# Two transformer blocks on one core: index scores in split precision, a re-dealt recurrence, shared PSUM banks and a reordered merge

## What is computed

```python
# the choice of keys in layer 0: 16 index heads of width 64
rel = jax.nn.relu(jnp.einsum('bqhd,bsd->bqhs', qii, k_idx) * (IDX_DIM ** -0.5))
score = jnp.einsum('bqhs,bqh->bqs', rel, wi)
_, sel = lax.top_k(score, n_keep)            # n_keep = 128
# the recurrence of the second block, per head and direction (a = running sum of log forget gates)
decay = jnp.exp(jnp.where(tri, diff, NEG_BIG))
scores = jnp.einsum('bhtd,bhjd,bhtjd->bhtj', qi, ki, decay)
s_new = exp(a_last) * s + jnp.einsum('bhjd,bhje->bhde', ki * jnp.exp(a_last - a), vi)
# the merge
up = jnp.einsum('blnw,nwd->blnd', ys, w_branch)
y = jnp.sum(jax.nn.sigmoid(gates) * up, axis=2) @ w_out
```

## Time and profile before

| what | value |
|---|---|
| median of 3 runs | 2319.14 us (2318.8 to 2319.22) |
| the profiled execution | 2319.98 us |
| its span, first to last instruction | 2318.1 us |
| busy: PE, PEld | 2298.1 us (99%), 1871.2 us (81%) |
| busy: DVE, ACT, POOL | 1416.7 us (61%), 1088.4 us (47%), 369.3 us (16%) |
| mean granted TensorE clock | 0.998 |
| moved by DMA | 233.02 MB, 101 GB/s on the mean |

### The profile page before, as it was taken

How to read it: one execution, slowest core, us unless ns; L and a number is a source line. 1 busy time by engine, 2 the same in 40 slices (tenths; PEclk the granted TensorE clock), 3 DMA queues, 4 the chain that set the end, 5 groups by cost and what they waited for, 6 DMA issues and landing times.

```text
span 2318.1 us, 30159 instructions
## 1 busy us (share of the span) xinstructions
PE 2298.1 (99%) x11870; PEld 1871.2 (81%) x11870; DVE 1416.7 (61%) x2304; ACT 1088.4 (47%) x1772; POOL 369.3 (16%) x280
## 2 busy tenths in 40 slices
PE   9999999999999999999999999999999999999998
PEld 7677788888877778888888878888887889888887
DVE  6886568848655546673676475557777336543443
ACT  5555555324435554542444366775555324441442
POOL 0002222202210001221222130001111222220222
PEclk9999999999999999999999999999999999999999
DMA  5122144533422213443343221011112432333231
GB/s 189 64 83 90 56 164 136 163 107 122 152 90 95 88 59 113 169 165 119 116 151 105 92 96 57 10 49 55 55 51 64 132 110 84 107 102 96 92 112 62
DMA packets 69932, 233.02 MB, mean 101 GB/s; under 512 B 8000, under 2 KB 10176, under 8 KB 69536
## 3 DMA queue, kind: packets, MB, share of 16 engines
q1 hardware_dynamic: 69792, 231.11, 30.5%
HBM read 224.18 MB, written 4.28 MB: 99 GB/s over the span
## 4 chain that ended last, share of the span: by engine, by line
PE 67%; DVE 2%; ACT 1%; issue 1%; DMA 0%; POOL 0%; DVEq 0%; SPq 0%; ACTq 0%
PE psum L478 18%; PE psum L480 18%; PE psum L479 18%; PE psum L1145 2%; PE psum L1164 2%; PE psum L1120 2%; PE psum L2063 1%; PE psum L2064 1%; PE psum L2065 1%; PE psum L1320 1%; PE psum L2646 1%; PE psum L1333 1%; PE psum L1348 1%; DVE wL L465 0%; DMA hf<-mixed 0%
## 5 line engine op out<-in xcount | busy, mean ns | idle before, releaser
L478 PE MATMUL psum<-hH,wH 128*128 128x512 f32 (+1 forms) x1904 | 759.8, 399 | 3.4 <-DVE hL L632 2.5
L480 PE MATMUL psum<-hH,wL 128*128 128x512 f32 (+1 forms) x1904 | 740.2, 389 | 0.0
L479 PE MATMUL psum<-hL,wH 128*128 128x512 f32 (+1 forms) x1904 | 739.2, 388 | 0.0
L465 DVE TENSOR_TENSOR wL<-raw,wH 128x1024 fp32r<-128x1024 f32 (+2 forms) x353 | 443.8, 1257 | 346.1 <-ACT wH L460 343.8
L460 ACT ACTIVATE wH<-raw 128x1024 fp32r<-128x1024 f32 (+2 forms) x353 | 363.3, 1030 | 490.3 <-PE psum L480 489.9
L478 PEld LDWEIGHTS psum<-hH,wH 128*128 128x128 f32 x1904 | 358.2, 188 | 86.9 <-issue 18.7
L480 PEld LDWEIGHTS psum<-hH,wL 128*128 128x128 f32 x1904 | 357.8, 188 | 74.4
L479 PEld LDWEIGHTS psum<-hL,wH 128*128 128x128 f32 x1904 | 358.5, 188 | 63.8 <-issue 0.7
L1897 POOL TENSOR_TENSOR sg<-sg,cv 128x512 f32<-128x512 f32 x66 | 95.1, 1440 | 676.9 <-ACT sg L1726 676.9
L478 PE MATMUL psum<-gH,wH 128*128 128x512 f32 x506 | 197.5, 390 | 0.0
L480 PE MATMUL psum<-gH,wL 128*128 128x512 f32 x506 | 196.8, 389 | 0.0
(11 more groups left out here) (379 smaller groups left out, 3313.7 us busy)
## 6 DMA issues: line engine op xcount, KB each, us to landing
raw<-in_up SPq DMA_DIRECT2D x132, 512.0 KB, 3.7
raw<-in_dn SPq DMA_DIRECT2D x48, 704.0 KB, 4.0
raw<-in_win SPq DMA_DIRECT2D x56, 512.0 KB, 3.7
mbuf<-in_wmod SPq DMA_DIRECT2D x48, 512.0 KB, 3.8
raw<-in_we SPq DMA_DIRECT2D x33, 512.0 KB, 3.7
raw<-in_wq SPq DMA_DIRECT2D x24, 512.0 KB, 3.6
tm<-toep SPq DMA_DIRECT2D x32, 256.0 KB, 4.3
raw<-in_wo SPq DMA_DIRECT2D x32, 256.0 KB, 2.6
```

Source lines behind the costliest of these rows:

```text
L465: ve.do.tensor_tensor(flat_of(wLb, n), flat_of(rawb, n), flat_of(wHb, n).bitcast(F), ALU.subtract).then_inc(*w_lo.up(n))
L478: pe.do.matmul(o, H[:, k, :], high(k), start=k == 0, stop=False)
L479: pe.do.matmul(o, H[:, k, :], low(k), start=False, stop=False)
L480: ins = pe.do.matmul(o, L[:, k, :], high(k), start=False, stop=k == kt - 1)
```

## The change

The index queries are kept as two float32r parts stacked on the partitions: for each head of a pair, `qiS` has the rounded part in 64 rows and the rest in the other 64; the key is kept as `kiH` and `kiL` with both halves of the rows the same. A score is then the sum of two float32r matmuls over 128 rows. ACT now copies each `qi` bank in two halves and DVE subtracts in two halves. The item order becomes query block 3, 1, 2, the items are issued one at a time, four ticks later; all 51 selection steps stand in attention steps 0 to 17; ACT scales both heads in steps 0 to 15. In the recurrence `cp` of a level stands behind the `w` of the level two further on, in the same step as its `use`; `yl` of the first four tiles stands after the last `use` of the last head; POOL's product at a head's end is an entry of its own (`yz`). Gate units take both banks, and a unit waits only for what last read its own bank. The 32-step attention of the second block yields once more in PE before its last products. In the merge, for the first 12 items, DVE's preparation of a weight stands behind the product. At the start PE runs five matmuls of zeros, and two waits for the small constants stand later.

```diff
@@ -230,7 +230,8 @@
-    qiA, qiB = [sb(f"qi{i}", [128, 4, S], at=mix_at + 16384 * i + 8192) for i in range(2)]
+    qiS = [sb(f"qi{c}", [128, 2, 384], R, at=mix_at + 3072 * c) for c in range(8)]
+    kiH, kiL = [sb(f"ki{x}", [128, S], R, at=mix_at + 24576 + 2048 * (x == "L")) for x in "HL"]
@@ -693,10 +694,10 @@
-        ac.wait_ge(*d_sm.at(0))
...
+        ac.wait_ge(*d_sm.at(0))
@@ -707,11 +708,11 @@
-        ve.wait_ge(*d_sm.at(0))
...
+        ve.wait_ge(*d_sm.at(0))
@@ -755,7 +756,7 @@
-        if x.kind in ("q", "k") or x.kind == "qi" and x.c % 2 == 0:
+        if x.kind in ("q", "k", "qi"):
@@ -770,19 +771,18 @@
-            out_ = [("ticks", 54)]
+            out_ = [("ticks", 58)]
...
-                out_ += [("ticks", 1)] + ([("scores", n)] if n % 2 == 0 else [])
-                out_ += [("index", n), ("ticks", 1)] + ([("keep", 1)] if n >= 11 else [])
+                out_ += [("ticks", 1), ("index", n), ("ticks", 1)]
...
-            per = [(4, 3)] * 10 + [(3, 3)] * 14 + [(2, 2)] * 6 + [(2, 1)] * 4 + [(0, 0)]
+            per = [(4, 3)] * 6 + [(3, 3)] * 18 + [(2, 2)] * 6 + [(2, 1)] * 4 + [(0, 0)]
...
-            keep = [("keep", 2 + s % 2)] if a.layer == 0 and s < 16 else []
+            keep = [("keep", 2 if s < 2 else 3)] if a.layer == 0 and s < 18 else []
...
-    def follow(a, ticks, steps, index=None, keep=None, scores=None):
+    def follow(a, ticks, steps, index=None, keep=None):
@@ -792,9 +792,6 @@
-            elif what == "scores" and scores is not None:
-                for i in range(n, n + 2):
-                    scores(i)
@@ -832,7 +829,7 @@
-                if i == 7 and x.kind == "qi" and x.c == 4:
+                if i == 3 and x.kind == "qi" and x.c == 5:
@@ -859,9 +856,10 @@
-                if x.c % 2:
-                    ac.wait_ge(*gemm.at(x.n))
-                    ac.do.activation(turned(qi(x.c)[:, late]), in_blocks(x.bank[:, late]), ACT.Copy).then_inc(*ev_a.up(x.n))
+                ac.wait_ge(*gemm.at(x.n))
+                for u in range(2):
+                    r_ = slice(64 * u, 64 * u + 64)
+                    ac.do.activation(turned(qiS[x.c][r_, u, :]), in_blocks(x.bank[r_, late]), ACT.Copy).then_inc(*ev_a.up((x.n, u)))
@@ -892,9 +890,11 @@
-                if x.c % 2 == 0:
-                    ve.wait_ge(*gemm.at(x.n))
-                    ve.do.tensor_copy(turned(qi(x.c)[:, late]), in_blocks(x.bank[:, late])).then_inc(*ev_v.up(x.n))
+                for u in range(2):
+                    r_, other = slice(64 * u, 64 * u + 64), slice(64 - 64 * u, 128 - 64 * u)
+                    ve.wait_ge(*ev_a.at((x.n, u)))
+                    ve.do.tensor_tensor(turned(qiS[x.c][other, u, :]), in_blocks(x.bank[r_, late]),
+                                        turned(qiS[x.c][r_, u, :].bitcast(F)), ALU.subtract).then_inc(*ev_v.up((x.n, u) if u == 0 else x.n))
@@ -964,6 +961,8 @@
+        ac.wait_ge(*ik_k.at(0))
+        ac.do.activation(kiH[:], kiT, ACT.Copy).then_inc(*ik_h.up(0))
@@ -983,11 +982,14 @@
+        ve.wait_ge(*ik_h.at(0))
+        ve.wait_ge(*ik_k.at(0))
+        ve.do.tensor_tensor(kiL[:], kiT, kiH[:].bitcast(F), ALU.subtract).then_inc(*ik_l.up(0))
...
-    index_items = [(1, c) for c in range(7)] + [(2, 0), (2, 1), (2, 2), (1, 7)] + [(2, c) for c in range(3, 8)]
-    index_items += [(3, c) for c in range(8)]
+    index_items = [(3, c) for c in range(7)] + [(1, 0), (1, 1), (1, 2), (3, 7)] + [(1, c) for c in range(3, 8)]
+    index_items += [(2, c) for c in range(8)]
@@ -1005,8 +1007,8 @@
-        pe.wait_ge(*ik_k.at(0))
-        pe.wait_ge(*(ev_v, ev_a)[c % 2].at(at["we", 1 + c]))
+        pe.wait_ge(*ik_l.at(0))
+        pe.wait_ge(*ev_v.at(at["we", 1 + c]))
@@ -1018,9 +1020,9 @@
-            r0 = 64 * u
-            ins = pe.do.matmul(bank[index_bank(n) + u][:, :W], qi(c)[r0:r0 + 64, i * 128:i * 128 + 128],
-                               kiT[r0:r0 + 64, :W], start=True, stop=True)
+            o, q_ = bank[index_bank(n) + u][:, :W], qiS[c][:, u, i * 128 - 128:i * 128]
+            pe.do.matmul(o, q_, kiH[:, :W], start=True, stop=False)
+            ins = pe.do.matmul(o, q_, kiL[:, :W], start=False, stop=True)
@@ -1052,7 +1054,7 @@
-        for i in range(1, 4):
+        for i in (3, 1, 2):
@@ -1147,6 +1149,8 @@
+            if s == wide_n:
+                yield
@@ -1298,6 +1302,10 @@
+    def shared(a, s):
...
+        return () if a.layer else (0, 1) if s < 16 else (1,)
@@ -1336,8 +1344,8 @@
-                pe.wait_ge(*at_p.at((a.key, q, 0)))
-                pe.wait_ge(*(ah_p if a.layer == 0 else at_p).at((a.key, q, 1)))
+                for u in range(2):
+                    pe.wait_ge(*(ah_p if u in shared(a, q) else at_p).at((a.key, q, u)))
@@ -1376,10 +1384,11 @@
-                p_ = Pr[:, s % 2, 1, :128 * (i + 1)]
-                h = 2 * (s // 4) + 1
...
-                ac.do.activation(p_, p_, ACT.Identity, scale=den[:, h:h + 1, i]).then_inc(*ah_p.up((a.key, s, 1)))
+                for u in shared(a, s):
+                    h = 2 * (s // 4) + u
+                    p_ = Pr[:, s % 2, u, :128 * (i + 1)]
+                    ac.do.activation(p_, p_, ACT.Identity, scale=den[:, h:h + 1, i]).then_inc(*ah_p.up((a.key, s, u)))
@@ -1406,7 +1415,9 @@
-                for u in range(1 if a.layer == 0 else 2):
+                for u in range(2):
+                    if u in shared(a, s):
+                        continue
@@ -2281,10 +2292,10 @@
-                    ac_high(ac, unit2("q", 1, c) + 3)
...
+                    ac_high(ac, unit2("q", 1, c) + 3)
@@ -2336,24 +2347,29 @@
+            def high(c):
+                return [("yh", c)] if h == 3 else []
...
-            out_ += [("tail", h - 1), ("yc", h - 1)] if h else []
+            out_ += [("tail", h - 1), ("yc", h - 1)] + ([("yz", h - 1)] if h < 3 else []) if h else []
...
-            out_ += [("use", h, 0), ("d", h, 3), ("w", h, 2), ticks_(2, 3), ("x", h, 3)]
-            out_ += [("use", h, 1), ("cp", h, 0), ("d", h, 4), ("w", h, 3), ("state", h, 1), *split(0), ticks_(4, 4), ("x", h, 4)]
-            out_ += [("use", h, 2), ("cp", h, 1), ("w", h, 4), ("d", h, 5), ("qe", h), *split(1), ticks_(2, 4), ("x", h, 5)]
-            out_ += [("use", h, 3), ("cp", h, 2), ("w", h, 5), ("d", h, 6), *split(2), ticks_(3, 4), ("x", h, 6)]
-            out_ += [("use", h, 4), ("cp", h, 3), ("w", h, 6), ("d", h, 7), ("qa", h), *split(3), ticks_(3, 4), ("x", h, 7)]
-            out_ += [("use", h, 5), ("cp", h, 4), ("w", h, 7), *opens(("fa", 0)), ticks_(2, 4)]
-            out_ += [("use", h, 6), ("cp", h, 5), *opens(("fv", 0), ("fa", 1), ("sc", 0)), ticks_(3, 3)]
-            out_ += [("use", h, 7), ("cp", h, 6), *opens(("fb", 0), ("ke", 0), ("kd", 0)), ticks_(2, 2), ("cp", h, 7), *split(4, 5), ticks_(1, 1)]
+            out_ += [("use", h, 0), ("d", h, 3), ("w", h, 2), ("cp", h, 0), ticks_(2, 3), ("x", h, 3)]
+            out_ += [("use", h, 1), ("d", h, 4), ("w", h, 3), ("cp", h, 1), ("state", h, 1), *high(0), ticks_(4, 4), ("x", h, 4)]
+            out_ += [("use", h, 2), ("d", h, 5), ("w", h, 4), ("cp", h, 2), ("qe", h), *high(1), ticks_(2, 4), ("x", h, 5)]
+            out_ += [("use", h, 3), ("d", h, 6), ("w", h, 5), ("cp", h, 3), *high(2), ticks_(3, 4), ("x", h, 6)]
+            out_ += [("use", h, 4), ("d", h, 7), ("w", h, 6), ("cp", h, 4), *high(3), ticks_(3, 4), ("x", h, 7)]
+            out_ += [("use", h, 5), ("w", h, 7), ("cp", h, 5), *opens(("fa", 0)), ticks_(2, 4)]
+            out_ += [("use", h, 6), ("qa", h), ("cp", h, 6), *opens(("fv", 0), ("fa", 1)), ticks_(3, 3)]
+            out_ += [("use", h, 7), ("cp", h, 7), *opens(("sc", 0), ("fb", 0), ("ke", 0), ("kd", 0)), ticks_(2, 2)]
+            out_ += [("yz", 2), *[("yl", c) for c in range(4)], *split(4, 5)] if h == 3 else []
+            out_ += [ticks_(1, 1)]
...
-            out_ += [("v6", h + 1), ("tsum", h)] if h < 3 else [("tsum", h), ("tail", h), ("yc", h)]
+            out_ += [("v6", h + 1), ("tsum", h)] if h < 3 else [("tsum", h), ("tail", h), ("yc", h), ("yz", h)]
@@ -2373,7 +2389,7 @@
-        return bank[1] if gate_of[n] in (0, 2) else bank[0]
+        return bank[1] if gate_of[n] in (0, 2, 4, 5, 6, 7, 9, 11) else bank[0]
@@ -2381,6 +2397,16 @@
+    def bank_reader(n, b):
...
+        every = [x for h in range(5) for x in fill_units(h)]
+        for p, what in reversed(every[:[x[0] for x in every].index(n)]):
+            if what in "fbv" and b:
+                return ev_a.at((p, "ctx"))
+            if (what == "g" and gate_bank(p) is bank[1]) == (b == 1):
+                return ev_a.at(p)
+        return None
@@ -2395,16 +2421,10 @@
-            if what == "g" and gate_of[n] < 4:
...
-                if gate_of[n]:
-                    pe.wait_ge(*g_read(*g_unit_before(g_unit_before(n)[0])))
-            elif (p := g_unit_before(n)) is not None:
-                pe.wait_ge(*g_read(*p))
+            if (p := bank_reader(n, 1 if what == "g" and gate_bank(n) is bank[1] else 0)) is not None:
+                pe.wait_ge(*p)
...
```

(35 more changed lines are left out.)

## The result

The changed kernel takes 2304.53 us (median of 4 runs, 2304.24 to 2305.04), the kernel before 2319.18 beside it (2318.80 to 2319.46): a ratio of 0.9937, 95% interval 0.9921 to 0.9953, a gain of 14.65 us. Forecast were 2308.8 us and a range from 2305.5; the direction and most mechanisms were right, but the gain is 1.4 times the 10.3 us of the sum and lies outside the range. The profiled execution took 2305.04 us (span 2303.0).

What follows compares the result with a forecast made beforehand. PE, busy 2298.1 of 2318.1 us, was taken as the bound. Terms summed to -10.3 us, from 2319.98 to 2309.7, less 0.84 for the median: 2308.8 us, range 2305.5 to 2314.0.

Steps and rivals of the forecast that it cites:

- Start: Kernel start: two more warm-up matmuls keep the clock up, so unit 1 starts earlier; -1.3 us.
- rival A: Kernel start: the clock falls all the same and the 1.3 us are lost, giving 2310.1 us; chance 10%.
- Index: Index scores: stacked float32r matmuls take 16.5 us where float32 blocks with mode changes took 20.3; -3.8 us.
- Selection: First attention steps: moved selection makes DVE lag, 0.7 us of waits gone and 1.2 new; +0.5 us, bounds -0.8 to +4.
- End of the wide attention: One yield puts a tick between PE's transposes and the products that waited 1.0 us for ACT; -0.9 us.
- Banks: Recurrence, three first heads: unit ends no longer wait for both banks; -1.2 us, bounds 0 and -1.8.
- Last head: Recurrence: earlier copy and later splits remove PE's three waits for L2804; 3.3 of 3.5 us gained.
- Merge: PE's 0.4 us wait behind L2930 shrinks, the product no longer behind a weight preparation; -0.3 us, at worst +0.5.
- B: First attention steps: DVE sets the pace in part, price 4 us more, 2312.8 us; chance 11%.
- C: Recurrence: waits move instead of going, 4.5 us there and 0.9 at wide attention's end don't come; 2314.2 to 2315; 8%.
- D: Attention steps: the chain of one step becomes serial through DVE and ACT, +14 us, so 2323; chance 3%.
- E: Index scores: each stacked matmul pays for its weight load, 18.0 us on top, 2326.8 us; chance 2%.

## Why the prediction was right and wrong

**Start (-1.3, measured -1.47):** right, and rival A did not happen: clock 1.00 from 8.6 on. The warm-up ended at 8.7 us, 0.3 beyond my estimate, and unit 1 began at 14.37 behind DVE's low weights, as said (14.4). But unit 0 was not fed by DVE at its end, as I had it: PE went through its 24 matmuls at 0.23 us each from 8.58 on, and DVE's last low tile was ready at 13.07, 0.6 us before the matmul that reads it (13.69).

**Index (-3.8; 3.5 by start to start):** right, and so is its split: I had 2.4 us for the mode and 1.4 for the pace, and the rows give 2.3 and 1.2. The emptying of the banks was hidden, as costed.

**Selection (+0.5; the stage came to -3.40 with the index, so about +0.1):** near in size. No wait of PE for the minimum is left; the new one is for ACT's scaling, which I had called free on the average of its stretch (27 of 50 us busy). DVE's lag, which I had forecast, is in it all the same: ACT stood 2.4 us for the minimum of that step.

**Query heads (0, measured -0.70, worth 0 to 0.7, by the median 0.45):** the step that is missing. The diff moved an instruction of ACT past a wait that the earlier trace rows would have shown with one more line of that view (0.88 us for the head square); I did not price it.

**End of the wide attention (-0.9, measured -1.05):** right.

**Banks (-1.2 with an upper bound of 1.8; measured 2.8 in the trace of the undone run, 3.2 by the medians):** the first step that failed. I counted "six such unit ends at about 0.2 us and two at 0.3" and then took two thirds. The count was right. The runs show the six at 0.27 and the two at 0.46, 2.6 us, and 0.2 more in the last head. I had written that a wait under 0.17 shows nowhere, and did not add the hidden part to the ends that I listed; then I took off a third for cover that was not there.

**Last head (-3.3; measured -4.4):** the second. Each of the three waits is longer from start to start than listed, by the same 0.16. In the kernel before:

```profile
1757.32 0.39 PE L480 MATMUL psum<-hH,wL 128*128 128x512 f32 x1
1759.23 1.13 PE L2646 MATMUL psum<-hf_pair 128*128 128x128 f32 x8 [1.52 <-DVE ssum L2804]
```

1.91 us where 0.23 is the pace, so 1.68, not 1.52; together 4.0, not 3.5, and the second matmul behind each wait starts another 0.08 us late. And the cause was named in part only. "The copy stands in DVE's queue behind a split" is true, but the splits alone are worth 1.1 us, the copy's place together with `qa` 2.5 (a microsecond of it in the other heads), which I had not costed apart, and POOL's product ahead of DVE's difference 1.1. My count of DVE's work, 24 us against PE's 24.7, held: no wait is left there.

**Merge (-0.3; measured -1.1, 1.6 by the median):** the third. The listed 0.4 us was one of several places (0.5 us from start to start); another, 0.3 us at the first units, is in no list.

**Range:** its low end was "every term at its good end", and the good ends were the listed waits. They were lower bounds. Rivals B, C and D did not happen, nor E.

## What to carry to other kernels

On an engine that is busy all the time, price a wait from the start of the matmul before it to its own start, less the fastest such distance, never from the listed idle time: here that adds 0.16 us to each listed one, and shows those that are not listed. If a queue is dealt anew, price every line of the diff that moves an instruction of any engine, POOL's too, and undo it by itself. An operation that is unusually long in one place (1.80 us for 0.68) is as good a lead as a wait.

## What the runs showed of the hardware that I had not expected

- A DVE subtraction of two SBUF operands, started 0.04 us after a POOL product of 1.30 us, took 1.80 us instead of 0.68, and 1.79 in the two runs that brought the product back. The order decides: in the kernel before, DVE's product L1848 takes 1.78 to 1.79 us the four times that POOL's sum (L527) began 0.09 to 0.36 us ahead of it, and 0.69 us the two times that POOL's began 0.04 us behind it, where POOL's took 1.80 instead of 1.32 to 1.59.
- A single float32 item between float32r matmuls costs 0.35 us over four float32r matmuls of the same work, at 512 columns as at 256; a block of two items costs 0.3 over eight.
- The granted clock: after PE stood 2.1 us the clock fell one microsecond later for 3.4 us; after 2.8 and 2.9 us PE came back at the lower level and worked 6.1 us at it; after 2.2 us ahead of unit 1 it fell 0.6 us later for 3.4 us.
- An early transfer of 322 KB landed 9.4 us after its issue in one profiled execution and 11.0 in another. In the second, with the waits for it at their old place, PE stood 2.2 us and lost 1.5 more through the clock. That this is what sets that execution apart from the four others of its kernel is likely but not shown.
